# One 512-column operand for the high weight half in two convolution FFNs, with the two results summed outside TensorE

## The chip, the cores and the metric

The kernel runs on one core of a Trainium2 chip. The metric is device time in microseconds (us), the median of several executions. TensorE multiplies matrices into PSUM, VectorE (DVE in the profile) and ScalarE (ACT) do elementwise work on PSUM and SBUF, GpSimd (POOL) does little here, and SyncE (SP) issues the loads of the weights.

## The reference

Two blocks run one after the other over 256 tokens of width 1024, all in fp32: attention and gated linear attention with two SwiGLU FFNs, then two layers of recurrent mixers, each followed by a convolution FFN. The change is in the two convolution FFNs:

```python
def conv_ffn(u, w_up, conv_w, conv_b, w_down):
    hdn = causal_dwconv(u @ w_up, conv_w) + conv_b
    gate, val = jnp.split(hdn, 2, axis=-1)
    return (jax.nn.silu(gate) * val) @ w_down
```

`w_up` is 1024 x 5632 (gate and value, 2816 columns each), `w_down` 2816 x 1024, and the convolution runs over three tokens, each channel by itself.

## The kernel before

Every fp32 product is made of three products of fp32r halves. A value is split into a high half (what the fp32r copy keeps) and a low half (the rest), and `three()` adds high x high, high x low and low x high in PSUM. Weights come in slots of 2048 columns per partition, six in a ring (`raw`). Each slot holds two pieces. ScalarE copies a piece to `whi` (`split_hi`, line 292), VectorE subtracts it from `raw` into `wlo` (`split_lo`, line 297), and TensorE uses both. `whi` and `wlo` are rings of six pieces: a copy waits until TensorE is through with the piece six before (`used`), and TensorE waits for `lo_done`. The activations were split before into `xh` and `xl`.

The four FFNs are `ffn0` to `ffn3`; `n` is the number, and the convolution FFNs are `n >= 2`. An FFN goes through its 2816 hidden columns in 11 groups (`GROUPS`, g = 0 to 10) of 256. For a group, `pe_gate_up` takes four pieces (the eight 128-row chunks `kc` of the input) and makes the gate and the value. In a convolution FFN the result has hidden columns on the partitions and tokens along the free side, in four parts: j (gate or value) and c (which 128 columns). `gate_or_up(n, q, j, c)` puts them into two PSUM banks, 4 and 5 for even groups, 6 and 7 for odd ones (q is the parity). Group 0 is made as rows instead, and turned by TensorE (line 922) after the first piece of group 1. So there are ten calls of `pe_gate_up` for each convolution FFN.

The hidden group is then made by `act_hidden` and `dve_hidden`: ScalarE applies the last tap and the bias (line 1018, four ACTIVATEs), VectorE adds two more taps (line 1045, eight SCALAR_TENSOR_TENSORs), ScalarE applies Silu (line 1024), VectorE multiplies (line 1051), ScalarE makes `hidh` (line 1061) and VectorE `hidl` (line 1065). `hid_lo` tells TensorE that a group is ready. `pe_down` multiplies it with two pieces of `w_down`, 12 products of 512 columns for each piece, and adds to PSUM banks 0 to 3.

The order on every engine is written out by hand. In the loop TensorE does gate and up of group g + 1, then down of group g. ScalarE and VectorE do, for group g, two splits, the hidden work, two splits, `hidh` or `hidl`, and two splits. The end of an FFN (`tail_at`, pieces b on) has its own order: gate and up of groups 9 and 10, down of group 8, and `pe_last_pieces`, which does the down products of groups 9 and 10 for the first 128 tokens (12 of group 9 first, and then those that need group 10), and then for the other 128.

## Time and profile before

| what | value |
|---|---|
| time, median of 3 runs | 1240.52 us (1240.47 to 1240.64) |
| the profiled execution: span from its first to its last instruction | 1238.8 us |
| TensorE matmuls | busy 1221.2 us (99%), 7393 instructions |
| VectorE | busy 841.0 us (68%), 1124 instructions |
| ScalarE | busy 677.6 us (55%), 987 instructions |
| chain of work that ended last | nearly all TensorE's own lines (305, 306 and 307, the three products) |

The profiled execution's own time is its span of 1238.8 us; the run's time has 1.7 us around it, which the profile does not show. A row of the timeline gives the start, the duration, the engine, the line, the operation, output and inputs, the tile's shape and how many instructions it joins, and in brackets the idle time before them and who ended it. A matmul's duration holds its way through the array, so the distance between two starts, not the duration, is what one costs in a full stream.

### The profile page before, as it was taken

What the parts mean: (1) busy time and instruction counts of PE and PEld (TensorE: products, weight loads), DVE (VectorE), ACT (ScalarE), POOL (GpSimd) and SP (SyncE); (2) the same over time, 40 slices, a digit from 0 to 9 for tenths busy, and PEclk for the clock granted to TensorE, in tenths of its full rate; (3) what the DMA queues carried; (4) which work ended last, traced back from release to release, by engine and by line L of the source; (5) the groups of instructions that cost most, each with busy time, mean ns of one, the idle gap of its engine ahead of it and who ended that gap; (6) DMA issues with size and microseconds to landing.
All of it is one profiled execution on the core that took longest, in us unless ns stands there. A gap on an engine that the chain in (4) does not pass through costs nothing. (4 is left out here: it accounts for less than half of the span.)

```text
span 1238.8 us, 19140 instructions
## 1 busy us (share of the span) xinstructions
PE 1221.2 (99%) x7393; PEld 1071.6 (86%) x7393; DVE 841.0 (68%) x1124; ACT 677.6 (55%) x987; POOL 50.8 (4%) x81
## 2 busy tenths in 40 slices
PE   8999999999999999999999999999999999999998
PEld 6888888887788888889998799999899887999997
DVE  5555457778654446767876777766868988866666
ACT  5444346464543335656635765554876657655455
POOL 0400000010000000101300000000000000000000
PEclk9999999999999999999999999999999999999999
DMA  9965555425555555544422565555553326555620
GB/s 336 266 221 176 172 203 176 137 69 170 194 175 171 199 203 204 173 153 126 147 69 86 185 209 183 171 172 201 190 198 106 120 86 220 171 185 188 203 102 35
DMA packets 139303, 209.14 MB, mean 169 GB/s; under 512 B 9941, under 2 KB 101331, under 8 KB 139234
## 3 DMA queue, kind: packets, MB, share of 16 engines
q1 hardware_dynamic: 136256, 199.39, 47.9%
q0 software_dynamic: 2832, 8.74, 2.5%
q8 instruction: 46, 0.75, 0.2%
q14 instruction: 23, 0.19, 0.0%
q10 hardware_dynamic: 146, 0.07, 0.0%
HBM read 207.12 MB, written 1.05 MB: 168 GB/s over the span
## 5 line engine op out<-in xcount | busy, mean ns | idle before, releaser
L297 DVE TENSOR_TENSOR wlo<-raw,whi 128x1024 fp32r<-128x1024 f32 (+1 forms) x380 | 443.6, 1209 | 46.9 <-ACT whi L292 46.3
L292 ACT ACTIVATE whi<-raw 128x1024 fp32r<-128x1024 f32 (+1 forms) x380 | 377.0, 1042 | 42.7 <-PE psum L307 42.3
L305 PE MATMUL psum<-whi,xh 128*128 128x512 f32 (+1 forms) x688 | 274.6, 399 | 3.4 <-DVE wlo L297 2.2
L305 PE MATMUL psum<-xh,whi 128*128 128x256 f32 (+1 forms) x944 | 268.2, 284 | 0.0
L307 PE MATMUL psum<-whi,xl 128*128 128x512 f32 (+1 forms) x688 | 267.0, 388 | 0.0
L307 PE MATMUL psum<-xh,wlo 128*128 128x256 f32 (+1 forms) x944 | 266.9, 283 | 0.0
L306 PE MATMUL psum<-xl,whi 128*128 128x256 f32 (+1 forms) x944 | 266.9, 283 | 0.0
L306 PE MATMUL psum<-wlo,xh 128*128 128x512 f32 (+1 forms) x688 | 266.4, 387 | 0.0
L306 PEld LDWEIGHTS psum<-xl,whi 128*128 128x128 f32 (+1 forms) x944 | 179.5, 190 | 1.2
L305 PEld LDWEIGHTS psum<-xh,whi 128*128 128x128 f32 (+1 forms) x944 | 179.4, 190 | 1.2
L307 PEld LDWEIGHTS psum<-xh,wlo 128*128 128x128 f32 (+1 forms) x944 | 179.4, 190 | 0.4
L305 PEld LDWEIGHTS psum<-whi,xh 128*128 128x128 f32 x688 | 129.3, 188 | 35.2 <-DVE wlo L297 4.3
L307 PEld LDWEIGHTS psum<-whi,xl 128*128 128x128 f32 x688 | 129.2, 188 | 27.2
L306 PEld LDWEIGHTS psum<-wlo,xh 128*128 128x128 f32 x688 | 129.5, 188 | 23.7
L305 PE MATMUL psum<-whi,hidh 128*128 128x512 f32 x352 | 137.5, 391 | 0.0
L306 PE MATMUL psum<-wlo,hidh 128*128 128x512 f32 x352 | 137.2, 390 | 0.0
L307 PE MATMUL psum<-whi,hidl 128*128 128x512 f32 x352 | 137.0, 389 | 0.0
L1045 DVE SCALAR_TENSOR_TENSOR arena<-psum,taps,arena 128x254 f32<-128x254 f32 (+1 forms) x176 | 74.7, 476 | 81.5 <-ACT arena L1018 77.4
L1065 DVE TENSOR_TENSOR hidl<-psum,hidh 128x512 fp32r<-128x512 f32 x22 | 15.2, 692 | 155.6 <-ACT hidh L1061 155.6
L1061 ACT ACTIVATE hidh<-psum 128x512 fp32r<-128x512 f32 x22 | 13.2, 598 | 172.0 <-PE psum L961 172.0
L1018 ACT ACTIVATE arena<-psum,taps 128x256 f32<-128x256 f32 x88 | 42.4, 562 | 90.2 <-PE psum L307 79.4
L307 PEld LDWEIGHTS psum<-whi,hidl 128*128 128x128 f32 x352 | 66.1, 188 | 13.9
(358 smaller groups left out, 1164.9 us busy)
## 6 DMA issues: line engine op xcount, KB each, us to landing
raw<-in_ffn_w_up SPq DMA_DIRECT2D x131, 512.0 KB, 5.2
raw<-in_ffn_w_down SPq DMA_DIRECT2D x88, 512.0 KB, 4.3
raw<-in_ffn_w_gate SPq DMA_DIRECT2D x43, 512.0 KB, 4.5
raw<-in_c_w_in SPq DMA_DIRECT2D x32, 512.0 KB, 4.6
raw<-in_ab_w_in SPq DMA_DIRECT2D x28, 512.0 KB, 4.7
raw<-in_w_in SPq DMA_DIRECT2D x18, 512.0 KB, 4.6
raw<-in_w_out SPq DMA_DIRECT2D x8, 512.0 KB, 4.4
raw<-in_ple_w_gate SPq DMA_DIRECT2D x8, 512.0 KB, 4.5
```

Source lines behind the costliest of these rows:

```text
L292: nc.scalar.activation(hi, r, ACT.Copy).then_inc(hi_done, 1)
L297: nc.vector.tensor_tensor(lo, r, hi.bitcast(F32), ALU.subtract).then_inc(lo_done, 1)
L305: nc.tensor.matmul(pe_out, sh, mh, start=start, stop=False, skip_group_check=True)
L306: nc.tensor.matmul(pe_out, sh, ml, start=False, stop=False, skip_group_check=True)
L307: return nc.tensor.matmul(pe_out, sl, mh, start=False, stop=stop, skip_group_check=True)
L1018: last = nc.scalar.activation(cg[:, q, j, c, :], gate_or_up(n, q, j, c), ACT.Identity, scale=tap(n, 2, f), bias=tap(n, 3, f))
L1045: last = nc.vector.scalar_tensor_tensor(y, gate_or_up(n, q, j, c)[:, 0:SEQ - lag], tap(n, k, g * 2 + (FC * j + c)), y, ALU.mult, ALU.add)
L1061: nc.scalar.activation(hidh[:, q], hidden_columns(q) if n < 2 else hp[:, q], ACT.Copy).then_inc(hid_hi, 1)
L1065: nc.vector.tensor_tensor(hidl[:, q], hidden_columns(q) if n < 2 else hp[:, q], hidh[:, q].bitcast(F32), ALU.subtract)\
```

## The change

For the convolution FFNs, `xh` and `xl` become the two halves of one tensor `xhl`, so that a 128 x 128 tile of the high weights is multiplied by both in one product of 512 columns. Its low 256 columns are high x high, its upper 256 columns high x low. The third product, low weights by `xh`, goes onto the low 256 columns as before. Each of the four parts of a group now has a PSUM bank of its own, so a group takes all of banks 4 to 7. ScalarE copies the upper halves of the four banks into `sums4` in SBUF (`act_low_part`, 1024 elements per partition) and VectorE adds the lower halves (`dve_sum`, 1024 elements). The taps read `sums4`. TensorE waits for `summed` of a group before it begins gate and up of the next one. Group 0 is turned into banks 2 and 3 and has no sum.

At the end of the FFN the order changes: gate and up of group 9, the first piece of down of group 8, gate and up of group 10, the second piece of down of group 8. The slots are cut accordingly (`sp_mixed` has half a slot of down and half of gate and up).

```diff
--- before.py
+++ after.py
@@ -105,8 +105,8 @@
         raw = sb("raw", [P, RING, SLOT])
         whi = sb("whi", [P, RING, PIECE], F32R)
         wlo = sb("wlo", [P, RING, PIECE], F32R)
-        xh = sb("xh", [P, KC, SEQ], F32R)
-        xl = sb("xl", [P, KC, SEQ], F32R)
+        xhl = sb("xhl", [P, KC, 2, SEQ], F32R)
+        xh, xl = xhl[:, :, 0, :], xhl[:, :, 1, :]
         hidh = sb("hidh", [P, 2, 2, SEQ], F32R)
         hidl = sb("hidl", [P, 2, 2, SEQ], F32R)
         h = sb("h", [P, NT, D])
...
@@ -264,10 +267,40 @@
                     sp_down(sp, s + 3 * half + 2, i, n, i * 2 + half)
             ffn_loop(sp, body)
             s += 3 * (GROUPS - 3)
+            if n >= 2:
+                sp_gate_up(sp, s, 0, n, GROUPS - 2)
+                sp_mixed(sp, s + 2, n, 0)
+                sp_gate_up_pieces(sp, s + 3, n, 2)
+                sp_mixed(sp, s + 4, n, 1)
+                for m in (1, 2):
+                    sp_down(sp, s + 4 + m, 0, n, GROUPS - 3 + m)
+                return
             for m in (0, 1):
                 sp_gate_up(sp, s + 2 * m, 0, n, GROUPS - 2 + m)
             for m in range(3):
                 sp_down(sp, s + 4 + m, 0, n, GROUPS - 3 + m)
+        def last_gate_up(n, j, k0, k1):
+            return FFN[n][j].rearrange("(k p) n -> p k n", p=P)[:, k0:k1, (GROUPS - 1) * GROUP:GROUPS * GROUP]
+        def sp_gate_up_pieces(sp, s, n, k0):
+            sp_slot(sp, s, 0, (4, 512), [((slice(None), slice(None), slice(256 * j, 256 * j + 256)), last_gate_up(n, j, k0, k0 + 4))
+                                         for j in range(2)])
+        def sp_mixed(sp, s, n, c):
+            sp.wait_ge(lo_done, 2 * (s - RING) + 2)
+            raw_halves = raw[:, s % RING, :].rearrange("p (h n) -> p h n", h=2)
+            row = FFN[n][2].rearrange("(f p) n -> p f n", p=P)[:, (GROUPS - 3) * 2 + c, :]
+            if c == 0:
+                sp.dma_start(raw_halves[:, 0, :], row).then_inc(mixed_down_in, 16)
+            view = raw_halves[:, 1 - c, :].rearrange("p (k j n) -> p k j n", k=2, j=2)
+            for j in range(2):
+                sp.dma_start(view[:, :, j, :], last_gate_up(n, j, 6 * c, 6 * c + 2)).then_inc(loaded[s % RING], 16)
+            if c == 1:
+                sp.dma_start(raw_halves[:, 1, :], row).then_inc(mixed_down_in, 16)
         def ffn_loop(eng, body):
...
@@ -880,9 +913,35 @@
-        def gate_or_up(n, q, j, c):
-            return psum[:, 4 + 2 * q + j, 256 * c:256 * c + 256]
+        def gate_or_up(j, c):
+            return bank(4 + 2 * j + c)
+        def first_columns(j, c):
+            return bank(2 + j, 256 * c, 256)
+        sums4 = arena[:, 4096:5120].rearrange("p (j c t) -> p j c t", j=2, c=2)
+        def sum_count(n, g):
+            return g + (n - 2) * (GROUPS - 1)
+        four_sums = sums4.rearrange("p j c t -> p (j c) t")
+        def act_low_part(act, n, g, p, i):
+            act.wait_ge(used, p + 2 * RING * i)
+            nc.scalar.activation(four_sums, psum[:, 4:8, SEQ:2 * SEQ], ACT.Copy).then_inc(low_copied, 1)
+        def dve_sum(dve, n, g):
+            dve.wait_ge(low_copied, sum_count(n, g))
+            nc.vector.tensor_tensor(four_sums, psum[:, 4:8, 0:SEQ], four_sums, ALU.add).then_inc(summed, 1)
+        def to_convolve(g, j, c):
+            return first_columns(j, c) if isinstance(g, int) and g == 0 else sums4[:, j, c, :]
         first_rows = arena[:, 5120:6144].rearrange("p (t n) -> p t n", t=NT)
...
@@ -942,9 +1003,11 @@
                     for c in range(2):
                         for j in range(2):
                             col = slice(256 * j + 128 * c, 256 * j + 128 * c + 128)
-                            last = three(gate_or_up(n, q, j, c), wh[:, kk, col],
-                                         wl[:, kk, col], xh[:, kc, :], xl[:, kc, :],
-                                         start=(kc == 0 and c == 0), stop=(kc == KC - 1))
+                            o = gate_or_up(j, c)
+                            nc.tensor.matmul(o, wh[:, kk, col], xhl[:, kc].rearrange("p h t -> p (h t)"), start=(kc == 0),
+                                             stop=False, skip_group_check=True)
+                            last = nc.tensor.matmul(o[:, 0:SEQ], wl[:, kk, col], xh[:, kc, :], start=False,
+                                                    stop=(kc == KC - 1), skip_group_check=True)
                 last.then_inc(used, 1)
                 if k in after_piece:
                     after_piece[k]()
...
@@ -984,10 +1047,15 @@
                     pe_down(pe, n, i * 2 + half, half, q + 4, i)
             ffn_loop(pe, body)
             b = tail_at(p)
-            for m in range(2):
-                between = {1: lambda: pe_hidden_turn(pe, n, GROUPS - 3 + m, m)} if n < 2 else {}
-                pe_gate_up(pe, n, GROUPS - 2 + m, 1 - m, b + 4 * m, 0, between)
-            pe_down(pe, n, GROUPS - 3, 0, b + 8, 0)
+            if n >= 2:
+                pe_gate_up(pe, n, GROUPS - 2, 1, b, 0)
+                pe_down(pe, n, GROUPS - 3, 0, b + 4, 0, pieces=(0,))
+                pe_gate_up(pe, n, GROUPS - 1, 0, b + 5, 0)
+                pe_down(pe, n, GROUPS - 3, 0, b + 8, 0, pieces=(1,))
+            else:
+                for m in range(2):
+                    pe_gate_up(pe, n, GROUPS - 2 + m, 1 - m, b + 4 * m, 0, {1: lambda: pe_hidden_turn(pe, n, GROUPS - 3 + m, m)})
+                pe_down(pe, n, GROUPS - 3, 0, b + 8, 0)
             if n < 2:
                 pe_hidden_turn(pe, n, GROUPS - 1, 0)
             pe.wait_ge(hid_lo, n * GROUPS + GROUPS - 1)
...
@@ -1007,6 +1075,8 @@
             first = isinstance(g, int) and g == 0
             if first and n >= 2:
                 act.wait_ge(*after(f"ffn{n}.columns"))
+            elif n >= 2:
+                act.wait_ge(summed, sum_count(n, g))
             else:
                 act.wait_ge(used, p + 2 * RING * i - (0 if first else 2))
             if n < 2:
...
@@ -1076,6 +1146,8 @@
                         split_hi(act, q + k, i=i)
                         if early == 4 and k == 1 and n >= 2:
                             act_first_row(act, n)
+                    if n >= 2 and not (isinstance(g, int) and g == 0):
+                        act_low_part(act, n, g, q - 2, i)
                     act_hidden(act, n, g, half, q, i)
                     for k in range(early, 4):
                         split_hi(act, q + k, i=i)
...
@@ -1084,15 +1156,26 @@
                         split_hi(act, q + k, shape=(2, D), i=i)
             ffn_loop(act, body)
             b, g = tail_at(p), GROUPS - 1
-            tail_splits = lambda *which: [split_hi(act, b + k) for k in which]
+            def tail_splits(*which):
+                for k in which:
+                    if n >= 2 and k in (4, 9):
+                        act.wait_ge(mixed_down_in, 32 * (n - 2) + (16 if k == 4 else 32))
+                    split_hi(act, b + k)
             tail_splits(0, 1)
+            if n >= 2:
+                act_low_part(act, n, g - 2, b - 2, 0)
             act_hidden(act, n, g - 2, 0, b, 0)
             tail_splits(2, 3)
             act_hid_hi(act, n, g - 2, 0, b, 0)
             tail_splits(4, 5, 6, 7)
+            if n >= 2:
+                act_low_part(act, n, g - 1, b + 4, 0)
             act_hidden(act, n, g - 1, 1, b + 6, 0)
             act_hid_hi(act, n, g - 1, 1, b + 6, 0)
             tail_splits(8, 9, 10, 11, 12)
+            if n >= 2:
+                act_low_part(act, n, g, b + 9, 0)
             act_hidden(act, n, g, 0, b + 10, 0, last_piece=None if n < 2 else b + 13)
             if n < 2:
                 tail_splits(13)
...
@@ -1122,13 +1207,19 @@
             b, g = tail_at(p), GROUPS - 1
             tail_splits = lambda *which: [split_lo(dve, b + k) for k in which]
             tail_splits(0, 1)
+            if n >= 2:
+                dve_sum(dve, n, g - 2)
             dve_hidden(dve, n, g - 2, 0, 0)
             tail_splits(2, 3)
             dve_hid_lo(dve, n, g - 2, 0)
             tail_splits(4, 5, 6, 7)
+            if n >= 2:
+                dve_sum(dve, n, g - 1)
             dve_hidden(dve, n, g - 1, 1, 0)
             dve_hid_lo(dve, n, g - 1, 1)
             tail_splits(8, 9, 10, 11, 12)
+            if n >= 2:
+                dve_sum(dve, n, g)
             dve_hidden(dve, n, g, 0, 0)
             if n < 2:
                 tail_splits(13)
```

The unshown hunks declare the semaphores, count `summed` in the two places that wait for it, put `to_convolve` where `gate_or_up` was read, and add `dve_sum` in VectorE's loop. Where the loop called `act_hidden` and `dve_hidden`, `act_low_part` and `dve_sum` now stand just ahead of them.

On TensorE, within a gate and up call, one chunk `kc` and the first two of the four parts read before:

```order
L305 MATMUL psum<-xh,whi 128x256
L306 MATMUL psum<-xl,whi 128x256
L307 MATMUL psum<-xh,wlo 128x256
L305 MATMUL psum<-xh,whi 128x256
L306 MATMUL psum<-xl,whi 128x256
L307 MATMUL psum<-xh,wlo 128x256
```

and now:

```order
L1007 MATMUL psum<-xhl,whi 128x512
L1009 MATMUL psum<-xhl,wlo 128x256
L1007 MATMUL psum<-xhl,whi 128x512
L1009 MATMUL psum<-xhl,wlo 128x256
L1007 MATMUL psum<-xhl,whi 128x512
L1009 MATMUL psum<-xhl,wlo 128x256
```

Three products of 256 columns, each with its own load of weights, have become one of 512 and one of 256.

On TensorE at the end of `ffn3`, the rows from the last product of gate and up of group 10 to the product that waits for group 10's hidden values (the wait for `hid_lo` in the last row), with the rows between left out, were before:

```order
L307 MATMUL psum<-xh,wlo 128x256
L305 MATMUL psum<-whi,hidh 128x512 [waits lo_done,hid_lo]
...
L305 MATMUL psum<-whi,hidh 128x512 [waits lo_done]
...
L305 MATMUL psum<-whi,hidh 128x512 [waits lo_done,hid_lo]
...
L305 MATMUL psum<-whi,hidh 128x512 [waits lo_done,hid_lo]
```

and are now:

```order
L1009 MATMUL psum<-xhl,wlo 128x256
L338 MATMUL psum<-whi,hidh 128x512 [waits lo_done,hid_lo]
L339 MATMUL psum<-wlo,hidh 128x512
...
L338 MATMUL psum<-whi,hidh 128x512 [waits lo_done,hid_lo]
L339 MATMUL psum<-wlo,hidh 128x512
...
L338 MATMUL psum<-whi,hidh 128x512 [waits lo_done,hid_lo]
```

Before, 36 products stand between gate and up of group 10 and that wait (24 of down of group 8 and 12 of group 9). Now 24 do: 12 of group 8's have moved ahead of gate and up of group 10, where the first product waits for `summed`.

On VectorE, at the first group of the end of `ffn3`, before:

```order
L297 TENSOR_TENSOR wlo<-raw,whi 128x1024 [waits hi_done] x2
L1045 SCALAR_TENSOR_TENSOR arena<-psum,taps,arena 128x255 [waits conv_mid]
L1045 SCALAR_TENSOR_TENSOR arena<-psum,taps,arena 128x255
L1045 SCALAR_TENSOR_TENSOR arena<-psum,taps,arena 128x254 [waits conv_one]
L1045 SCALAR_TENSOR_TENSOR arena<-psum,taps,arena 128x254
```

and now:

```order
L330 TENSOR_TENSOR wlo<-raw,whi 128x1024 [waits hi_done] x2
L940 TENSOR_TENSOR arena<-psum,arena 128x1024 [waits low_copied]
L1115 SCALAR_TENSOR_TENSOR arena<-arena,taps 128x255 [waits conv_mid]
L1115 SCALAR_TENSOR_TENSOR arena<-arena,taps 128x255
L1115 SCALAR_TENSOR_TENSOR arena<-arena,taps 128x254 [waits conv_one]
```

The sum stands between the splits and the taps of its group, and the taps of both engines now come behind it (ScalarE's wait for `summed`).

## Rows read from the trace of the kernel before

**Rows 1.** The page's section 1: busy time, share and instructions.

```profile
PE 1221.2 (99%) x7393; PEld 1071.6 (86%) x7393; DVE 841.0 (68%) x1124; ACT 677.6 (55%) x987; POOL 50.8 (4%) x81
```

**Rows 2.** Waits of TensorE from 700 us on: total, times, longest.

```profile
PE psum L313 <- DVE arena L2874: 0.4, 1, 0.4
PE psum L305 <- DVE xl L328: 0.3, 1, 0.3
PE psum L305 <- DVE wlo L297: 0.2, 1, 0.2
```

**Rows 3.** TensorE's timeline in the loop of `ffn2`: start, duration, instruction.

```profile
729.64 0.28 PE L305 MATMUL psum<-xh,whi 128*128 128x256 f32 x1
...
741.15 0.40 PE L305 MATMUL psum<-whi,hidh 128*128 128x512 f32 x1
...
742.54 0.39 PE L305 MATMUL psum<-whi,hidh 128*128 128x512 f32 x1
...
746.62 0.28 PE L305 MATMUL psum<-xh,whi 128*128 128x256 f32 x1
```

**Rows 4.** The same timeline, where group 0 is turned.

```profile
714.67 1.03 PE L922 MATMUL psum<-const,arena 128*128 128x128 f32 x8
715.46 0.36 PE L305 MATMUL psum<-xh,whi 128*128 128x256 f32 x1
```

**Rows 5.** Groups by line and form: busy, mean ns, idle before.

```profile
L2190 DVE TENSOR_TENSOR arena<-psum,small 128x1024 f32<-128x1024 f32 x3 | 3.6, 1222 | 0.8 <-POOL small L344 0.7
...
L2552 ACT ACTIVATE arena<-psum 128x1024 f32<-128x1024 f32 x3 | 3.0, 1020 | 0.3 <-PE psum L2216 0.3
```

**Rows 6.** Timelines of three engines, one group in the loop of `ffn2`.

```profile
775.11 0.40 PE L305 MATMUL psum<-whi,hidh 128*128 128x512 f32 x1
...
775.53 1.93 ACT L1018 ACTIVATE arena<-psum,taps 128x256 f32<-128x256 f32 x4 [4.91 <-PE psum L307]
...
781.09 2.35 DVE L297 TENSOR_TENSOR wlo<-raw,whi 128x1024 fp32r<-128x1024 f32 x2
...
787.63 1.23 DVE L297 TENSOR_TENSOR wlo<-raw,whi 128x1024 fp32r<-128x1024 f32 x1 [0.18 <-ACT whi L292]
```

**Rows 7.** VectorE and TensorE, the first group of the loop of `ffn3`.

```profile
1076.94 2.35 DVE L297 TENSOR_TENSOR wlo<-raw,whi 128x1024 fp32r<-128x1024 f32 x2
...
1080.90 0.28 PE L305 MATMUL psum<-xh,whi 128*128 128x256 f32 x1
```

**Rows 8.** ScalarE's and VectorE's timelines at the end of `ffn3`.

```profile
1205.72 1.93 ACT L1018 ACTIVATE arena<-psum,taps 128x256 f32<-128x256 f32 x4 [4.70 <-PE psum L307]
...
1217.24 1.93 ACT L1018 ACTIVATE arena<-psum,taps 128x256 f32<-128x256 f32 x4 [0.80 <-PE psum L307]
...
1211.74 0.69 DVE L1065 TENSOR_TENSOR hidl<-arena,hidh 128x512 fp32r<-128x512 f32 x1 [0.70 <-ACT hidh L1061]
1212.69 5.77 DVE L297 TENSOR_TENSOR wlo<-raw,whi 128x1024 fp32r<-128x1024 f32 x5 [0.26 <-ACT whi L292]
...
1223.73 0.69 DVE L1065 TENSOR_TENSOR hidl<-arena,hidh 128x512 fp32r<-128x512 f32 x1 [1.10 <-ACT hidh L1061]
```

**Rows 9.** TensorE's timeline at the end of `ffn3`.

```profile
1217.04 0.40 PE L305 MATMUL psum<-whi,hidh 128*128 128x512 f32 x1
...
1225.23 0.39 PE L305 MATMUL psum<-whi,hidh 128*128 128x512 f32 x1
...
1233.16 0.39 PE L307 MATMUL psum<-whi,hidl 128*128 128x512 f32 x1
```

**Rows 10.** Timelines of VectorE and TensorE at the start: a hand-over.

```profile
11.78 1.23 DVE L297 TENSOR_TENSOR wlo<-raw,whi 128x1024 fp32r<-128x1024 f32 x1
...
13.16 0.47 PE L305 MATMUL psum<-whi,xh 128*128 128x512 f32 x1 [0.33 <-DVE wlo L297]
```

**Rows 11.** Windows after the last matmul: us, busy by engine, PEclk (granted clock), DMA.

```profile
1237.00:1238.00 1.00, 0.00 (x0) 0.00 (x0) 0.00 (x0) 0.00 (x0) 0.00 (x0) 1.00 0.98 369
1238.00:1238.80 0.80, 0.00 (x0) 0.00 (x0) 0.00 (x0) 0.00 (x0) 0.00 (x0) 0.70 0.01 3
```

More of the change, by code:

```diff
@@ L165, in build @@
         conv_all = sem("conv_all")
+        low_copied = sem("low_copied")
+        summed = sem("summed")
+        mixed_down_in = sem("mixed_down_in")
         params = sem("params")
@@ L1017, in act_hidden @@
                     f = g * 2 + (FC * j + c)
-                    last = nc.scalar.activation(cg[:, q, j, c, :], gate_or_up(n, q, j, c),
+                    last = nc.scalar.activation(cg[:, q, j, c, :], to_convolve(g, j, c),
                                                 ACT.Identity, scale=tap(n, 2, f), bias=tap(n, 3, f))
@@ L1114, in body @@
                             dve_first_row(dve, n)
+                    if n >= 2 and not (isinstance(g, int) and g == 0):
+                        dve_sum(dve, n, g)
                     dve_hidden(dve, n, g, half, i)
```

9 lines of the change are left out of this document (6 added, 3 removed).

## The prediction

> **What bounds the kernel now.** I read the page's busy times first [rows 1]: TensorE is busy for 1221.2 of 1238.8 us, VectorE for 68% and ScalarE for 55%. A busy matmul engine can still hide waits, so I read what TensorE waits for from 700 us on, where both convolution FFNs lie: three waits, 0.9 us in all, none inside these FFNs' loops [rows 2]. So the part of the program that changes is bound by TensorE's own stream. The reader is to see two things. A nanosecond off this stream is a nanosecond off the time. And any new wait of TensorE is added in full, since there is no idle time that it could fill.
>
> **What the products cost.** The timeline gives the distance of starts, which counts here [rows 3]. One gate and up call, 96 products of 256 columns, takes 741.15 - 729.64 = 11.51 us, 119.9 ns each. The 24 products of 512 columns behind it take 746.62 - 741.15 = 5.47 us, 228 ns each; in the last stretch 35 of them take 1233.16 - 1225.23 = 7.93 us, 226.6 ns each [rows 9]. The granted clock is 1.00 of 2.4 GHz in this program until the last 0.8 us [rows 11], so the columns alone are 106.7 and 213.3 ns. Both forms carry about 13 ns more, a price of each product with its weight load.
>
> **The gain.** Three products of 256 columns (359.7 ns) become one of 512 and one of 256: 226.6 + 119.9 = 346.5 ns, or 347.8 ns with the other row. One price of 13 ns goes. A call has 32 such triples (8 chunks by 4 parts), so it falls by 0.38 to 0.42 us, and there are 10 calls in each of two FFNs. 640 triples by 12.5 ns are 8.0 us. Bounds: 640 by 11.9 = 7.6 and 640 by 13.2 = 8.5 us. The alternation of the two forms is not in the trace; the first six products of 512 behind a call stand 232 ns apart (741.15 to 742.54, [rows 3]), and if all 512-column products of the pairs were so, the gain would be 5.2 us. I take 8.0.
>
> **The work that is added.** ScalarE's copy reads 1024 elements of PSUM; the nearest row of that form takes 1.02 us. VectorE's sum of 1024 with one operand in PSUM is like the row of 1.22 us [rows 5]. With two hand-overs at some 0.05 us, which I assume, the taps of every group come 2.35 us later than now. That they now read SBUF in place of PSUM I count as nothing; cases 4 and 5 take it from both sides. The question is who is late by it. There are three places.
>
> *In the loop it is hidden.* Now, ScalarE begins the taps 0.42 us after the last product of the call (775.11 to 775.53), and VectorE begins the two splits behind the hidden work at 781.09 [rows 6]. The third piece of the next call is ready at 781.09 + 1.22 = 782.31. After the change it is ready at 784.66, 784.81 with the 0.15 us that VectorE's hand-over to TensorE takes (11.78 + 1.23 to 13.16, [rows 10]). TensorE wants it after 24 down products and two pieces of the shorter call, at 775.11 + 5.47 + 5.55 = 786.13: 1.3 us to spare. The sum itself is done 0.42 + 1.02 + 0.05 + 1.22 = 2.7 us behind the call, and the next call, which waits for it because a group now fills all four banks, begins 5.47 us behind: 2.8 us to spare. VectorE's last split of the group ends at 788.86 now [rows 6] and at 791.2 then; the next call ends at 775.11 + 16.6 = 791.7. So VectorE keeps up, with about 1.6 us until the next sum.
>
> *In the first group of each loop it is not quite.* There the taps start late, since ScalarE has four splits before them, and VectorE begins the next splits at 1076.94 [rows 7]. The third piece is ready at 1078.16 + 2.35 - 0.10 (the call is earlier by a piece's share, 0.10) + 0.15 = 1080.56. TensorE now wants it at 1080.90 [rows 7], and then at 1080.90 - 0.41 - 0.20 = 1080.29. Cost 0.27 us, twice: 0.5 us.
>
> *At the end of each FFN it stands on the path.* TensorE needs the hidden values of group 10 as soon as the down products before them are through. Now 36 products stand between, 1225.23 - 1217.04 = 8.19 us [rows 9], and `hidl` is ready at 1223.73 + 0.69 = 1224.42 [rows 8], 0.8 us early. The change lengthens the chain and takes 12 products out of its cover. They have moved ahead of the last gate and up call, where they cover the wait for the sum of group 9: 2.73 us against 0.20 + 1.02 + 0.05 + 1.22 + 0.15 = 2.64, so nothing is waited there. For group 10, counted from TensorE's last gate and up product:
> - ScalarE starts 0.20 us later (1217.04 to 1217.24).
> - The chain in group 9, which nothing held up, takes 1211.74 + 0.69 - 1205.72 = 6.71 us [rows 8].
> - Copy and sum add 2.35 us.
> - VectorE is late by 0.2: its five splits end at 1212.69 + 5.77 = 1218.46 [rows 8], 12.74 us behind the start of group 9's chain, so then at 15.09. The copy of group 10 ends at 2.73 + 11.10 + 1.02 = 14.85.
> - The hand-over to TensorE is 0.15 us.
>
> This is 9.6 us, against 24 products of 5.46 us. TensorE waits 4.15 us. The same code ends `ffn2`: 8.3 us for both.
>
> **The sum.** -8.0 + 0.5 + 8.3 = +0.8 us on the span of 1238.8. Nothing in what lies around it changes, so the same goes onto the median: 1240.52 + 0.8 = 1241.3 us. What the shorter stream gives is taken back by two waits. A measurement of this kernel can tell about 0.2%, 2.5 us, from no change.
>
> **A rule weighed against the rows.** From 700 us on TensorE waits for 0.4 us at most [rows 2] until its last product. After that one (1233.16 + 0.39, [rows 9]) the granted clock was 1.00 to 1238.0 and fell in the last 0.8 us, to a mean of 0.70 [rows 11]: about 4.8 us of idleness at the fall. The new waits leave it idle for about 4.0 us. By the row alone the clock stays, and the sum is as above. The Trainium skill, "TensorE: Matmul & The Clock Gate", section "HAM oscillation — how this bites in real kernels", says that kernels whose TensorE waits between bursts fall back to the lower clock and start each burst cold. By that rule both waits would be followed by slow products, and the time would be that of the second case below. No row here shows a wait of this length with work behind it.
>
> **The rivals.**
> 1. *As summed*, 0.47. Its own range is 1239.7 (gain 8.5, waits 3.8 each) to 1243.4 (gain 6.5, waits 4.4 each, 0.3 in each first group).
> 2. *The clock falls in one or both waits*, 0.17. At 1.2 GHz 512 columns take 213 ns more. If it comes back after the 12 products behind the wait, a fall costs 2.6 us: 1243.9 for one, 1246.5 for two.
> 3. *The weight load sets the pace of the 256-column products*, 0.12. The eight turns of 128 columns start 0.10 us apart (714.67 to 715.46, [rows 4]), twice their columns, so a load of 128 x 128 costs about that much. A product of 256 columns has hardly more than that to hide it. Behind a 512-column product the next load is fully covered; if the 13 ns fell away there, a pair would take 227 + 107 = 334 ns, the gain would be 16.5 us and the time 1232.8. Against it: the products of 512 columns have ample cover and carry the same 13 ns. The Trainium skill, the same page, section "LDWEIGHTS (loading the stationary operand)", puts the load at the number of columns divided by 1.2 GHz, 107 ns; the turns agree.
> 4. *VectorE becomes the bound*, 0.09, the other side. Its work in a group grows by the sum's 1.22 us, and the period falls from 16.98 us (729.64 to 746.62, [rows 3]) by 0.4. It decides from where the chain in the loop is longer by 1.3 us more than I worked out (register work between its waits, slower reads). At 1.8 us more, each of 18 groups costs 0.5: 1250.
> 5. *The end is cheaper*, 0.15. Taps read from SBUF may be shorter. At 0.1 us for each of eight, a wait is 3.3 us and the time 1239.7; below 1238 it takes 1.7 us off each chain.
>
> **How the numbers follow.** Faster by over 0.2% are case 3 and 0.06 of case 5: 0.18. Slower are 0.16 of case 2, case 4 and 0.04 of case 1: 0.29. The rest, 0.53, is the same. The range of 1237.0 to 1247.0 leaves out case 3, most of case 4 and a little of case 5, together 0.2.
>
> **What would show it.** In the new trace a gate and up call should take 11.1 us, with pairs of 347 ns. TensorE should wait about 4 us for VectorE's `hidl` at the end of each convolution FFN and 0.3 us for `wlo` in the first group, and not in the loop. The copy should take 1.0 us, the sum 1.2. A granted clock below 1.00 behind the two waits means case 2, pairs of 334 ns case 3, waits for `wlo` in every group case 4. I am wrong in the large if the two waits are under 2.5 us or over 5.5.

## The result, and the profile after

The changed kernel takes 1248.06 us (median of 5 executions, 1247.88 to 1249.71) against 1240.64 of the kernel before on the same chip. The ratio is 1.0063, with a 95% interval of 1.0049 to 1.0077: slower by 7.4 us. The forecast was 1241.3 us with a range of 1237.0 to 1247.0. It was 6.8 us too low, and the result lies 1.1 us outside the range.

The profiled execution is one of the longer two: 1249.71 us, span 1247.9 us, mean granted clock 0.995. The profile page's first section, beside [rows 1]:

```profile
PE 1222.8 (98%) x6753; PEld 1040.4 (83%) x6753; DVE 865.1 (69%) x1144; ACT 699.4 (56%) x1007; POOL 50.8 (4%) x81
```

TensorE has 640 products fewer and is busy for 1.6 us more. Its waits from 700 us on (total, times, longest), beside [rows 2]:

```profile
PE psum L338 <- DVE hidl L1135: 7.4, 2, 3.7
PE psum L346 <- DVE arena L2965: 0.4, 1, 0.4
PE psum L338 <- DVE xhl L361: 0.3, 1, 0.3
PE psum L338 <- DVE wlo L330: 0.2, 1, 0.2
```

The first line is the one that is new: TensorE waits for VectorE's `hidl` at the end of each FFN. No line is a wait for a sum (it would name `arena` L940), and `wlo` has not grown.

**The products.** TensorE's timeline in the loop of `ffn2`, which answers to [rows 3]; the columns are start, duration, instruction:

```profile
746.78 0.39 PE L1007 MATMUL psum<-xhl,whi 128*128 128x512 f32 x1
...
748.06 0.28 PE L1009 MATMUL psum<-xhl,wlo 128*128 128x256 f32 x1
748.18 0.40 PE L1007 MATMUL psum<-xhl,whi 128*128 128x512 f32 x1
748.41 0.28 PE L1009 MATMUL psum<-xhl,wlo 128*128 128x256 f32 x1
748.53 0.40 PE L1007 MATMUL psum<-xhl,whi 128*128 128x512 f32 x1
...
758.07 0.40 PE L338 MATMUL psum<-whi,hidh 128*128 128x512 f32 x1
...
763.57 0.39 PE L1007 MATMUL psum<-xhl,whi 128*128 128x512 f32 x1
```

The call takes 758.07 - 746.78 = 11.29 us, a pair 353 ns (748.18 to 748.53), and the 24 products of down 5.50 us, where they took 5.47. So the period is 16.79 us in place of 16.98: a gain of 0.19 us a group, where 0.40 was forecast.

**The added work.** Groups by line and form (busy, mean ns of one, idle time before and its releaser), beside [rows 5]:

```profile
L1088 ACT ACTIVATE arena<-arena,taps 128x256 f32<-128x256 f32 x80 | 41.6, 591 | 30.0 <-DVE arena L940 30.0
...
L940 DVE TENSOR_TENSOR arena<-psum,arena 128x1024 f32<-128x1024 f32 x20 | 24.5, 1224 | 32.3 <-ACT arena L935 32.3
L935 ACT ACTIVATE arena<-psum 128x1024 f32<-128x1024 f32 x20 | 20.5, 1025 | 64.0 <-PE psum L1009 64.0
```

Copy 1.02 us and sum 1.22 us, as the nearest rows said. A tap of ScalarE that reads SBUF takes 591 ns, where L1018 before took 562. In the loop there was room for all of it. VectorE's and TensorE's timelines, for the group of [rows 6]:

```profile
776.12 1.23 DVE L940 TENSOR_TENSOR arena<-psum,arena 128x1024 f32<-128x1024 f32 x1 [1.82 <-ACT arena L935]
...
783.25 2.35 DVE L330 TENSOR_TENSOR wlo<-raw,whi 128x1024 fp32r<-128x1024 f32 x2
```

```profile
786.00 0.40 PE L1007 MATMUL psum<-xhl,whi 128*128 128x512 f32 x1
```

The sum ends at 777.35, 3.0 us before the next call begins (780.36). The third piece is ready with the first of the two splits, at about 784.5 and 0.15 for the hand-over, and its first product starts at 786.00: 1.4 us to spare.

**The end of `ffn3`.** ScalarE's, VectorE's and TensorE's timelines, which answer to [rows 8, 9]:

```profile
1223.32 1.03 ACT L935 ACTIVATE arena<-psum 128x1024 f32<-128x1024 f32 x1 [0.92 <-PE psum L1009]
1224.38 1.23 DVE L940 TENSOR_TENSOR arena<-psum,arena 128x1024 f32<-128x1024 f32 x1
1225.64 2.08 ACT L1088 ACTIVATE arena<-arena,taps 128x256 f32<-128x256 f32 x4 [1.29 <-DVE arena L940]
1226.77 3.50 DVE L1115 SCALAR_TENSOR_TENSOR arena<-arena,taps 128x255 f32<-128x255 f32 x8 [1.16 <-ACT arena L1088]
...
1231.76 0.69 DVE L1135 TENSOR_TENSOR hidl<-arena,hidh 128x512 fp32r<-128x512 f32 x1 [0.70 <-ACT hidh L1131]
```

```profile
1228.40 0.39 PE L340 MATMUL psum<-whi,hidl 128*128 128x512 f32 x1
1232.50 0.69 PE L338 MATMUL psum<-whi,hidh 128*128 128x512 f32 x1 [3.72 <-DVE hidl L1135]
1232.99 0.63 PE L339 MATMUL psum<-wlo,hidh 128*128 128x512 f32 x1
1233.42 0.63 PE L340 MATMUL psum<-whi,hidl 128*128 128x512 f32 x1
...
1235.98 0.43 PE L340 MATMUL psum<-whi,hidl 128*128 128x512 f32 x1
1236.25 0.40 PE L338 MATMUL psum<-whi,hidh 128*128 128x512 f32 x1
```

The last product of gate and up gives way to down at 1223.12, and `hidl` is ready at 1232.45. TensorE would have gone on at 1228.40 + 0.23 = 1228.63 and goes on at 1232.50: 3.87 us. Behind the wait the starts of two products stand 0.43 us apart (1232.99 to 1233.42) instead of 0.227, down to 1235.98. The windows name the cause; their column PEclk is the granted clock, the third value from the end. First the end of `ffn2`, then that of `ffn3`:

```profile
880.00:882.00 2.00, 0.00 (x0) 0.00 (x0) 1.20 (x3) 1.13 (x2) 0.00 (x0) 0.77 0.00 0
882.00:884.00 2.00, 1.72 (x4) 1.43 (x5) 2.00 (x3) 1.98 (x3) 0.00 (x0) 0.50 0.00 0
884.00:886.00 2.00, 2.00 (x6) 1.52 (x6) 1.63 (x2) 0.69 (x1) 0.00 (x0) 0.50 0.71 200
...
1230.00:1232.00 2.00, 0.00 (x0) 0.00 (x0) 1.20 (x3) 0.89 (x2) 0.00 (x0) 1.00 0.00 0
1232.00:1234.00 2.00, 1.50 (x4) 1.21 (x5) 1.59 (x2) 1.03 (x1) 0.00 (x0) 0.66 0.00 0
1234.00:1236.00 2.00, 2.00 (x7) 1.51 (x6) 0.00 (x0) 0.00 (x0) 0.00 (x0) 0.50 0.00 0
```

The clock fell to 0.50, 1.2 of 2.4 GHz, at both waits. The shares place the fall: 0.77 in the window from 880 us puts it at 881.1, 2.5 us after TensorE's last product had ended; 0.66 in the window from 1232 us puts it at 1232.6, just after TensorE had begun again. The clock stayed low for some 13 products in `ffn2` and 9 in `ffn3`.

**Where the time went.** From the first product of group 1's gate and up to the end of the last gate and up call the changed kernel is shorter by 1.82 us in each FFN, the 12 moved products taken off; twice, 3.6 us. The two ends, counted from the last call over the same products, are longer by 6.7 and 5.7 us: 7.75 us are the waits, 4.65 is lost by the products behind them, most of it to the clock (e2 below splits it). A longer wait for the first weights at the start (0.7 us after 0.3), which has nothing to do with the change, closes the account: -3.6 + 7.75 + 4.65 + 0.4 = 9.2 us of the spans' 9.1. The median's 7.4 us would fit the same terms with less slow time, which isn't shown: the other executions weren't profiled.

### The profile page after: what moved, and what is told of

Read it like the earlier page. It is cut to its first block and busy times, and to the rows that moved or that the text cites. A ratio compares the mean times of both kernels' runs of the same rounds, so it can differ in the third digit from the quotient of the medians.

```text
span 1247.9 us, 17938 instructions
## 1 busy us (share of the span) xinstructions
PE 1222.8 (98%) x6753; PEld 1040.4 (83%) x6753; DVE 865.1 (69%) x1144; ACT 699.4 (56%) x1007; POOL 50.8 (4%) x81
## 3 DMA queue, kind: packets, MB, share of 16 engines
HBM read 207.12 MB, written 1.05 MB: 167 GB/s over the span
## 5 line engine op out<-in xcount | busy, mean ns | idle before, releaser
L338 PE MATMUL psum<-whi,xhl 128*128 128x512 f32 (+1 forms) x688 | 274.7, 399 | 3.7 <-DVE wlo L330 2.7
L340 PE MATMUL psum<-whi,xhl 128*128 128x512 f32 (+1 forms) x688 | 266.9, 388 | 0.0
L339 PE MATMUL psum<-wlo,xhl 128*128 128x512 f32 (+1 forms) x688 | 266.5, 387 | 0.0
L1007 PE MATMUL psum<-xhl,whi 128*128 128x512 f32 x640 | 226.6, 398 | 0.0
L1009 PE MATMUL psum<-xhl,wlo 128*128 128x256 f32 x640 | 179.6, 281 | 0.0
L338 PEld LDWEIGHTS psum<-whi,xhl 128*128 128x128 f32 x688 | 129.3, 188 | 35.3 <-DVE wlo L330 4.3
L340 PEld LDWEIGHTS psum<-whi,xhl 128*128 128x128 f32 x688 | 129.2, 188 | 27.3
L339 PEld LDWEIGHTS psum<-wlo,xhl 128*128 128x128 f32 x688 | 129.5, 188 | 23.7
L1007 PEld LDWEIGHTS psum<-xhl,whi 128*128 128x128 f32 x640 | 120.2, 188 | 29.4
L1009 PEld LDWEIGHTS psum<-xhl,wlo 128*128 128x128 f32 x640 | 120.8, 189 | 0.8
L338 PE MATMUL psum<-xhl,whi 128*128 128x256 f32 (+1 forms) x304 | 87.1, 286 | 0.0
L339 PE MATMUL psum<-xhl,whi 128*128 128x256 f32 (+1 forms) x304 | 85.8, 282 | 0.0
L340 PE MATMUL psum<-xhl,wlo 128*128 128x256 f32 (+1 forms) x304 | 85.8, 282 | 0.0
```

The source lines that it names most:

```text
L338: nc.tensor.matmul(pe_out, sh, mh, start=start, stop=False, skip_group_check=True)
L339: nc.tensor.matmul(pe_out, sh, ml, start=False, stop=False, skip_group_check=True)
L340: return nc.tensor.matmul(pe_out, sl, mh, start=False, stop=stop, skip_group_check=True)
L1007: nc.tensor.matmul(o, wh[:, kk, col], xhl[:, kc].rearrange("p h t -> p (h t)"), start=(kc == 0), stop=False, skip_group_check=True)
L1009: last = nc.tensor.matmul(o[:, 0:SEQ], wl[:, kk, col], xh[:, kc, :], start=False, stop=(kc == KC - 1), skip_group_check=True)
```

## The experiments

Two things had come out otherwise than forecast: the products' gain was half of what was worked out, and the clock fell. The theory was that these two, with the two waits that had been forecast, explain the time. Its rivals were that the order at the end, the copy and sum, or the new layout cost something that the list of waits does not show. Each experiment ran beside the kernel before on the same chip: 1240.92 us for the first four (e1 to e4), 1240.29 for the next four (e5 to e8), 1240.81 for the last two. Ahead of `ffn2` all of them do the same work, and yet their profiles differ there, even where the clock stays at 1.00, by up to 1.6 us, nearly all of it at the start: the first product that waits for `wlo` starts at 13.16 us before, at 13.57 after and at 12.21 in e1. So profiles are also compared from `ffn2` on, from the first product of group 1's gate and up (712.21 us in the changed kernel) to the start of the last product: 521.4 us before and 530.0 after.

**The old order at the end (e1).** The table of the end is undone, on TensorE and in SyncE's loads:

```diff
-                pe_down(pe, n, GROUPS - 3, 0, b + 4, 0, pieces=(0,))
-                pe_gate_up(pe, n, GROUPS - 1, 0, b + 5, 0)
-                pe_down(pe, n, GROUPS - 3, 0, b + 8, 0, pieces=(1,))
+                pe_gate_up(pe, n, GROUPS - 1, 0, b + 4, 0)
+                pe_down(pe, n, GROUPS - 3, 0, b + 8, 0)
```

> The changed kernel with the order of the end as before (gate and up of groups 9 and 10, then all of down of group 8). TensorE then waits in two places per FFN in place of one: about 2.6 us for the sum of group 9 with nothing to cover it, and for hidl of group 10 the chain of 9.35 us less 36 products of 8.2 us, about 1.2 us. Both together are 3.8 us, as long as the one wait now. Theory A (the length of the single wait matters, because the granted clock falls in a wait of 4 us and the products behind it are slow, about 4.3 us in both FFNs): no fall of the clock, about 4 us faster than the changed kernel, 1244. Rival B (only the sum of the waiting counts): as the changed kernel, 1248.

Measured: 1247.54 us, ratio 1.0049 (1.0033 to 1.0066). The profiled execution is the shortest, 1244.25 us with a clock of 0.999. TensorE's waits in it:

```profile
PE psum L999 <- DVE arena L932: 4.7, 2, 2.4
PE psum L330 <- DVE hidl L1126: 2.1, 2, 1.1
```

By this list the one wait of 3.7 us has become two, 2.35 us for the sum of group 9 and 1.05 us for `hidl`. By the starts of the products, as the 3.87 us were counted, they are 2.53 and 1.22 us, 3.75 for each FFN, so the old order saves hardly any waiting. The seven executions fall into three levels: three lie at 1244.3 to 1245.0 us with a mean clock of 0.999, two at 1247.5 and 1247.6 with 0.997, and two at 1249.8 and 1250.0 with 0.995. With the clock kept, the account is 1240.92 - 3.6 + 7.5 = 1244.8 us, and the lowest level fits it. The stretch from `ffn2` on takes 525.9 us in the profiled execution, 4.5 more than before. The median is where rival B had it, the lowest level where theory A had it. By their mean clock the other levels are one and two falls, which no profile shows; e10 below tests it. If they lie in the waits, even a wait of 2.5 us can lose the clock.

**Idle products in the wait (e2).** The kernel after, with 16 products on zeros, behind the sum of group 10, ahead of the wait for the hidden values:

```diff
+                        if X in ("ffn2", "ffn3"):
+                            pe.wait_ge(summed, sum_count(int(X[3]), GROUPS - 1))
+                            for _ in range(16):
+                                nc.tensor.matmul(bank(4), zero_r[:, :], xhl[:, 0].rearrange("p h t -> p (h t)"), start=True, stop=True,
+                                                 skip_group_check=True)
```

> The changed kernel with 16 idle products of 512 columns (zero weights, into bank 4, after the sum of group 10) put into the wait for hidl of group 10 at the end of each convolution FFN. They take about 3.6 of the 3.9 us, so the wait for VectorE stays as long, but TensorE works in it. Theory A: the granted clock stays 1.00, the 12 products behind the wait take 227 ns each, and the time falls by about 4.3 us to about 1244. Rival B: no change, or slower by what the idle products overrun.

Measured: 1245.55 us, ratio 1.0035 (1.0022 to 1.0048). Eight of nine executions have a clock of 0.999. The end of `ffn2` in the profiled one, timeline and window:

```profile
878.02 3.79 PE L859 MATMUL psum<-xhl,zero_r 128*128 128x512 f32 x16
881.90 0.50 PE L338 MATMUL psum<-whi,hidh 128*128 128x512 f32 x1
882.24 0.40 PE L339 MATMUL psum<-wlo,hidh 128*128 128x512 f32 x1
```

```profile
882.00:884.00 2.00, 2.00 (x9) 1.63 (x10) 2.00 (x2) 1.98 (x3) 0.00 (x0) 1.00 0.00 0
```

The useful product comes just as late as before, 3.88 us (878.02 to 881.90). What is gone is the fall: 1.00 in the window that read 0.50, and starts 0.23 us apart. From `ffn2` on the profiled execution takes 526.0 us, 4.0 less than the changed kernel: the two ends are shorter by 2.5 and 1.6 us. That is what the clock cost. The other 0.5 us of the 4.65 is lost at the full clock too, by the first products behind a wait, which stand 0.34 us (881.90 to 882.24) and then 0.24 us apart. So the clock is a cost of its own here, and the change with the clock kept is 4.6 us slower than before (526.0 against 521.4), as is this run's median (1245.55 against 1240.92). The expectation of 1244 had counted this half microsecond as the clock's.

**The last two groups as before (e3, and again as e8).** Groups 1 to 8 as in the change, groups 9 and 10 with three products of 256 and no sum, the old order at the end:

```diff
+        def as_before(g):
+            return isinstance(g, int) and g >= OLD_FROM
...
+                            if as_before(g):
+                                last = three(two_banks(q, j, c), wh[:, kk, col], wl[:, kk, col], xh[:, kc, :], xl[:, kc, :],
+                                             start=(kc == 0 and c == 0), stop=(kc == KC - 1))
+                                continue
```

> Groups 1 to 8 of each convolution FFN as in the changed kernel, groups 9 and 10 as before (three products of 256 columns, two banks, no copy and no sum) and the order of the end as before. The lengthened chain then never meets the end. Theory A: no waits for hidl, the clock stays, and 16 of the 20 calls are 0.2 us shorter: about 3 us faster than the kernel before, 1237.5. Rival B (the copy and the sum hurt in the loop as well, by port or queue effects that the waits don't show): the kernel before or slower, 1240.5 and more.

> The kernel that has groups 1 to 8 as in after and the last two groups and the end as before, once more, beside the grouped one on the same chip. Theory A (the waits at the ends were all that spoiled the change, and each new call is 0.22 us shorter): 16 x 0.22 = 3.5 us less, less some 0.5 us for the longer chain in the first groups, about 1238. Theory B (the 0.25% of the first run came from which executions lost the clock for a while): the times of both kernels overlap mode by mode, within 0.5 us.

Measured: 1238.15 us, ratio 0.9975 (0.9963 to 0.9987), and again 1237.88 us, 0.9978 (0.9968 to 0.9987). The waits at the ends are gone, and the kernel is faster than before, in e8 by 2.8 us from `ffn2` on (518.6 us). That settles that everything which makes the change slow sits in the last two groups and the order at the end. The same copies, sums and banks in the loop cost no wait. Of e8's forecasts the first held (about 1238).

The first of these two shows something else. Its profiled execution, 1240.93 us, lost the clock ahead of `ffn2`, where the code is that of before, and came to `ffn2` 3.0 us late (714.79 us for 711.79). The second line is the kernel before in the same stretch:

```profile
660.00:670.00 10.00, 9.23 (x56) 7.16 (x56) 3.60 (x7) 5.82 (x11) 0.00 (x0) 0.66 0.17 56
```

```profile
660.00:670.00 10.00, 9.23 (x76) 7.71 (x76) 4.42 (x10) 6.91 (x12) 0.00 (x0) 1.00 0.18 57
```

TensorE is idle for the same 0.77 us in both, its only wait in this stretch (the wait before it, of 0.57 us, ends at 656.2), yet the clock is 0.66 in one and 1.00 in the other; 9.23 us of busy time are 56 products in one and 76 in the other. The profile of e6 has 0.66 in the same stretch. The kernel before probably has such executions too: 6 of its 26 beside the first four experiments lay at 1244.0 to 1244.4 us with a mean clock of 0.996, 3 us above most of the others; none of them was profiled.

**Four and four (e4).** In each chunk the four products of 512 columns stand together, then the four of 256:

```diff
+                    for half in range(2):
+                        for c in range(2):
+                            for j in range(2):
...
+                                if half == 0:
+                                    nc.tensor.matmul(o, wh[:, kk, col], xhl[:, kc].rearrange("p h t -> p (h t)"), start=(kc == 0),
```

> The changed kernel with the order of the products in a chunk changed: first the four products of 512 columns, then the four of 256. The pairs cost 353 ns in the changed kernel where 347 were predicted. Theory C (it is the alternation that costs 6 ns): a call falls from 11.29 to about 11.1 to 11.2 us, and 20 of them by 2 to 4 us: 1244 to 1246. Rival D (the 512-column product with activations as the moving operand costs 6 ns more wherever it stands): 1248, a call of 11.29 us.

Measured: 1247.54 us, ratio 1.0050 (1.0031 to 1.0068); the clock fell in every execution (mean clock 0.994 to 0.997), so the total, which was forecast at 1244 to 1246, tells little. The call does. TensorE's timeline:

```profile
746.47 1.07 PE L1009 MATMUL psum<-xhl,whi 128*128 128x512 f32 x4
747.38 0.64 PE L1012 MATMUL psum<-xhl,wlo 128*128 128x256 f32 x4
747.85 1.09 PE L1009 MATMUL psum<-xhl,whi 128*128 128x512 f32 x4
...
757.67 0.40 PE L338 MATMUL psum<-whi,hidh 128*128 128x512 f32 x1
```

The call takes 11.20 us instead of 11.29: 350 ns for one of each form.

**Two products of 256 (e5).** The product alone is undone; banks, copy, sum, order and waits stay:

```diff
-                            nc.tensor.matmul(o, wh[:, kk, col], xhl[:, kc].rearrange("p h t -> p (h t)"), start=(kc == 0),
+                            nc.tensor.matmul(o[:, 0:SEQ], wh[:, kk, col], xh[:, kc, :], start=(kc == 0),
+                                             stop=False, skip_group_check=True)
+                            nc.tensor.matmul(o[:, SEQ:2 * SEQ], wh[:, kk, col], xl[:, kc, :], start=False,
```

> The kernel of after, but the 512-column product of each pair is given as two products of 256 columns that write the same two halves of the same bank: the product is all that is undone; banks, copy, sum, order and waits stay. Theory A (the pair of 512 and 256 columns costs 353 ns, three of 256 cost 360): a gate and up call takes 11.51 us again, where after has 11.29, and the time is 20 x 0.22 = 4.4 us above after's, near 1252. Theory B (the call is short of what was forecast because of the new operand's layout or the bank that each part now has for itself, and not because of the product's form): the call stands above 11.6 us, since those stay and the product's gain goes.

Measured, one execution: 1250.54 us. The call takes 11.51 us and down behind it 5.47 again (TensorE's timeline):

```profile
746.84 0.28 PE L1007 MATMUL psum<-xhl,whi 128*128 128x256 f32 x1
...
758.35 0.40 PE L338 MATMUL psum<-whi,hidh 128*128 128x512 f32 x1
```

So layout and banks cost nothing that this profile shows, and the whole 0.22 us a call is the product's. The total is some 2 us less than forecast. One reason stands in the windows: the clock fell at only one of the two waits, which are alike, 3.9 us each. The first, behind which TensorE began again at 883.87, and the second, behind which it began again at 1234.96:

```profile
884.00:886.00 2.00, 2.00 (x7) 1.62 (x8) 2.00 (x2) 1.98 (x3) 0.00 (x0) 0.74 0.00 0
886.00:888.00 2.00, 2.00 (x6) 1.51 (x6) 1.22 (x2) 1.01 (x4) 0.00 (x0) 0.50 0.96 283
```

```profile
1234.00:1236.00 2.00, 1.04 (x5) 0.87 (x6) 1.79 (x2) 1.46 (x2) 0.00 (x0) 1.00 0.00 0
```

The fall came at 885.0, 1.1 us after TensorE had begun again.

**All of 512 columns (e6).** The low weight half too takes both token halves, which adds the product of the two low halves:

```diff
-                            last = nc.tensor.matmul(o[:, 0:SEQ], wl[:, kk, col], xh[:, kc, :], start=False,
+                            last = nc.tensor.matmul(o, wl[:, kk, col], xhl[:, kc].rearrange("p h t -> p (h t)"), start=False,
```

> The kernel of after, with the low weight half too multiplied by both token halves as one 512-column operand; this adds the product of the two low halves. A call is then 64 products of 512 columns with no alternation. Theory A (a product of 512 columns costs 233 ns where products of 256 stand among those just ahead of it, and 227 where none do): the call takes 64 x 227 = 14.5 us. Theory B (with this operand a product of 512 costs 233 ns in any company): 64 x 233 = 14.9 us. The time of the whole is 20 x 3.2 to 3.6 us above after's, 1312 to 1320 us, with the waits at the two ends as they are.

Measured, one execution: 1316.85 us. The timeline:

```profile
750.46 0.39 PE L338 MATMUL psum<-whi,hidh 128*128 128x512 f32 x1
...
755.90 0.39 PE L1007 MATMUL psum<-xhl,whi 128*128 128x512 f32 x1
...
770.41 0.39 PE L338 MATMUL psum<-whi,hidh 128*128 128x512 f32 x1
```

The call is (770.41 - 755.90) / 64 = 226.7 ns a product, and down, with no products of 256 ahead of it, falls from 5.47 to 5.44 us, also 226.7 ns each. So the new operand is not what makes the product dear: 226.7 ns holds, but only in a stream of 512-column products.

The changed kernel, e4, e5 and e6 have two waits of 3.9 us each in their profiles, eight in all. The clock fell at seven of them, and not at the second of e5. Of the seven falls four came during the wait, with TensorE idle for 2.3 to 3.1 us, and three up to 1.3 us after it had begun again. One of each, the first wait of e6 (TensorE idle from 912.97 to 916.75) and the second of e4 (idle until 1230.81):

```profile
914.00:916.00 2.00, 0.00 (x0) 0.00 (x0) 1.21 (x3) 0.66 (x2) 0.00 (x0) 0.82 0.00 0
```

```profile
1232.00:1234.00 2.00, 2.00 (x7) 1.58 (x6) 0.00 (x0) 0.03 (x1) 0.00 (x0) 0.53 0.00 0
```

The falls are at 915.3 and at 1232.1 us.

**Grouping with the old ends (e7 in fours, e9 in eights).** The loop of e4, and one over the two chunks of a piece, in the kernel of e3.

> Groups 1 to 8 as in after, but four products of 512 and then four of 256 in each chunk; groups 9 and 10 and the order at the end as in the kernel before. Theory A (what is left of the gain is lost at changes between the two forms): a new call takes 11.20 us as in the grouped run, 0.09 us less than with pairs, 16 calls, so 1.4 us less than the same kernel with pairs: near 1236.7 us, 0.34% under before. Theory B (grouping brings nothing that can be told in the time): as the kernel with pairs, 1238.2.

> As the grouped kernel with the last two groups as before, but in groups of eight: the eight products of 512 columns of a piece (two chunks) and then its eight of 256. At 226.7 and 120.0 ns each a call would take 11.09 us; in fours it takes 11.20, in pairs 11.29. Theory A (each return from 256 to 512 columns costs a fixed sum, 15.6 ns in fours): four returns in place of eight, 11.15 us, and 16 x 0.05 = 0.8 us less than in fours, near 1234.5 us. Theory B (a product of 512 is dear while products of 256 stand within six places ahead of it, 33 ns behind a long run of them, as in the kernel before): 4 x 33 ns, 11.22 us, and no gain.

Measured: in fours 1235.22 us, ratio 0.9960 (0.9948 to 0.9972); in eights 1235.62 us, 0.9956 (0.9943 to 0.9970). TensorE's timeline in eights:

```profile
746.26 1.98 PE L1007 MATMUL psum<-xhl,whi 128*128 128x512 f32 x8
748.08 1.12 PE L1010 MATMUL psum<-xhl,wlo 128*128 128x256 f32 x8
...
757.41 0.40 PE L331 MATMUL psum<-whi,hidh 128*128 128x512 f32 x1
```

The call takes 11.15 us, as theory A of e9 had it: 11.09 us would be the sum of the bare prices, and 0.11 us are lost over eight returns to 512 columns (fours, 11.20 us), 0.06 us over four. In fours the median lies 2.7 us under e8 of the same chip, where 1.4 was forecast. But 1.1 us of the difference between the profiled ones arose ahead of `ffn2`, where the code is the same; from `ffn2` on they take 517.0 and 518.6 us, and the shortest executions, 1235.05 and 1236.57, are 1.5 apart. The medians of fours and eights can't be told apart for the same reason: e7's profile is 1.2 us ahead at the start of `ffn2` (710.64 and 711.88). From there on eights take 516.2 us, 0.8 less than fours, as forecast, and the shortest executions (1234.24 and 1235.05) are 0.8 apart as well. With one profile of each, on two chips, that is a fit and not a proof.

**Idle products with the old order (e10).** e1 with 9 idle products ahead of the wait for the sum and 4 ahead of that for `hidl`:

```diff
+                if isinstance(g, int) and g == GROUPS - 1:
+                    for _ in range(9):
+                        nc.tensor.matmul(bank(0), zero_r[:, :], xhl[:, 0].rearrange("p h t -> p (h t)"), start=False, stop=False,
```

> The kernel of after with the order of before at the end, whose executions lay at 1244.5, 1247.6 and 1249.9 us, with idle products (zeros, 512 columns, added to a bank of down) before both of its waits: 9 ahead of the wait of 2.4 us for the sum of group 9, and 4 ahead of the wait of 1.1 us for the hidden values. Theory A (the upper two levels are executions in which the clock fell in one of these waits): nearly all executions at 1244.3 to 1244.8. Theory B (they come from elsewhere in the program): three levels as before, median near 1247.5.

Measured: 1245.52 us, ratio 1.0043 (1.0029 to 1.0057). Four of five executions lie at 1244.8 to 1245.6 us with a clock of 0.999 or 1.000, one at 1248.4 with 0.997; e1 had four of seven above 1247. That fits theory A, that e1's upper levels were falls in its waits, but one of five against four of seven is too few to show it, and a fall ahead of `ffn2`, as in e3, costs the same 3 us. The level is 1 us above the forecast of 1244.3 to 1244.8, which came from e1's lowest executions. That microsecond lies at the very start: the first product that waits for `wlo` starts at 13.48 us here and at 12.21 in e1, and from `ffn2` on both take 525.9 us. The fifth execution may be a fall elsewhere; it wasn't profiled.

## Why the prediction was wrong

The mechanism of the two waits was right. So was the sign of the sum, but +0.8 us is too small to be told from no change, and slower had a chance of only 0.29. The sum should have been +4.1 with the clock kept (+4.6 with the products just behind the waits, e2), and the measured +7.4 needs the clock as well. By its own steps:

- *What bounds the kernel*: right. TensorE's stream was the bound, and each new wait was added in full.
- *The gain, 8.0 us*: the first step that failed, a term taken at more than twice its size. The sum took 226.6 + 119.9 ns for a pair. These are prices of uniform streams. The call's own neighbour said otherwise: the first six products of 512 behind a call stood 232 ns apart [rows 3], and the prediction worked out 5.2 us from that row and set it aside as a bound. A pair took 353 ns, 233 + 120, so that bound was nearly the right price: 4.4 us in the calls (20 by 0.22). Of these 0.6 are lost where down follows (5.50 us for 5.47) and some 0.2 in the first groups. Measured: 3.6 us.
- *Copy, sum, hand-overs*: 1.02, 1.22 and 0.04 us, as costed. The taps came 2.3 us later, forecast 2.35.
- *The loop, hidden*: right. The third piece was ready 1.4 us before it was wanted (forecast 1.3), the sum 3.0 us before the next call (2.8).
- *The first groups, 0.5 us*: no wait for `wlo` appeared in either. In `ffn3` VectorE began the two splits 2.37 us later than before, as costed, and the third piece was ready at about 1085.7 us. But TensorE wanted it only at 1085.84, some 0.4 us later than forecast, because down and the calls had given back less.
- *The wait for group 9's sum, nothing*: right.
- *The waits for group 10, 4.15 us each*: 3.87. From the last call to the product behind the wait it took 9.38 us (1223.12 to 1232.50), not 9.6. Start, copy and sum came as costed, and taps to `hidl` took 6.81 us (1225.64 to 1232.45) for 6.71, with ScalarE's slower taps. But VectorE's lateness of 0.2 us did not come, and the hand-over was 0.05 us, not 0.15. The cover was 5.51 for 5.46. What the sum had at nothing is the 0.5 us that the products just behind the two waits lose at the full clock (e2).
- *The clock*: the second step that failed. "By the row alone the clock stays" compared 4.0 us of idleness with the 4.8 us of one fall at the program's end [rows 11]. One fall at 4.8 us shows that such an idle time is enough, not that a shorter one isn't. In the first wait the clock was down after 2.5 us, and at the second it fell just behind the wait. The mean clock of all five executions (0.995 to 0.997) says that each lost it; how often, only the profiled one shows. The case had a chance of 0.17. Its price of 2.6 us a fall was right for the first (2.5) and 1 us too high for the second (1.6, by e2). The Trainium skill, "TensorE: Matmul & The Clock Gate", section "HAM oscillation — how this bites in real kernels", says that bursts behind such waits start cold. The windows agree, 0.50 behind both; behind the second wait of e5, just as long, it was 1.00.
- *The rivals*: weight loads that pace the products of 256 would have given pairs of 334 ns, and no run showed them. VectorE as the bound: no wait in the loop. A cheaper end: 0.28 us a wait (3.87 for 4.15), a sixth of what that case needed to come below 1238; and ScalarE's taps from SBUF were dearer, not cheaper.

Not settled: why a product of 512 columns costs 6 ns more when products of 256 stand among those just ahead of it. The runs show how much and when, not the mechanism. Why one wait of 3.9 us keeps the clock and seven alike do not is open as well.

## What to carry to other kernels

Take an instruction's price from a stretch with the mix of forms that the new code will have; where the trace shows the same form at two prices, the one beside the other form is the one to sum. A wait of some microseconds on a matmul engine that is otherwise full costs its length and, at seven of the eight waits of 3.9 us here, the slow products behind it: cost it with both. Where it can't be avoided, idle products in it can keep the clock (e2), but they don't shorten it. Before two profiles are compared, subtract what differs in the stretch that both have in common. A rework that lengthens a chain belongs where the chain is covered; leaving it out of the last two groups turned 0.6% slower into 0.25% faster, and grouping the products made that 0.4%.

## What the runs showed of the hardware

- A product of 512 columns took 226.7 ns in a stream of its own kind (e6) and 233 ns with 256-column products among the ones just ahead (behind a long run of them, six stood at 232). Changes of form cost 0.20 us in a call with 32 returns to 512 columns (11.29 us for 11.09), 0.11 us with eight and 0.06 us with four.
- The clock's fall is not decided by the idle time alone. Of eight profiled waits of 3.9 us seven lost it and one, of two alike in one execution, kept it (e5). Four falls came with TensorE idle for 2.3 to 3.1 us, three only after it had begun again, the latest 1.3 us after. A stretch with waits of 0.8 us or less lost it in two profiled executions (e3, e6) and kept it in others. By the mean clock, four executions of seven with waits of 2.5 and 1.2 us (e1) lost it somewhere. The Trainium skill, the page named above, section "What's actually happening", says of the other side, the rise, that the same kernel shows it at other places from run to run. These falls vary in the same way.
- At the lower clock products of 512 columns stood 427 ns apart, and the full clock came back while they ran: after some 13 products in one place and 9 in the other.
- Sixteen idle products on zeros in each wait of 3.9 us kept the clock at 1.00 in the profiled execution (e2).
